# Hybrid macaron layer on one core: seven more seven-product units in the two feed-forward blocks, and the hidden tiles' splits moved

## The reference

```
h = x + 1/2 * SwiGLU_1(RMSNorm(x))
u = RMSNorm(h); P = u @ W_in
h = h + W_out(sigmoid(G_A) * (RWKV7(P) @ L_A) + sigmoid(G_B) * (DeltaNet(P) @ L_B))
h = h + CrossAttention(RMSNorm(h), RMSNorm(mem))
h = h + 1/2 * SwiGLU_2(RMSNorm(h))
y = RMSNorm_final(h)

SwiGLU(x) = (silu(n @ w_gate) * (n @ w_up)) @ w_down,  n = RMSNorm(x)
w_gate, w_up: 2048 x 5632     w_down: 5632 x 2048
```

## Time and profile before

| what | us |
|---|---|
| median of 3 runs | 2585.56 (2580.27 to 2589.16) |
| profiled execution, its own time | 2583.24 |
| its span, first to last instruction | 2581.5 |
| around the span | 1.74 |

### The profile page before, as it was taken

One profiled execution on the slowest core, in us unless ns is written; L12 is line 12 of the kernel. 1 busy time (PEld: TensorE's weight loads), 2 busy tenths in 40 slices (PEclk: granted clock), 3 DMA queues, 4 the chain that ended last, 5 costly groups with the idle time before them and its releaser, 6 DMA issues.

```text
span 2581.5 us, 34288 instructions
## 1 busy us (share of the span) xinstructions
PE 2553.0 (99%) x13611; PEld 2097.4 (81%) x13611; DVE 2019.9 (78%) x2403; ACT 1365.1 (53%) x1602; POOL 188.4 (7%) x346
## 2 busy tenths in 40 slices
PE   8999999999999999999999999999999999999998
PEld 7888888888888777878788888888888888888887
DVE  6999998887767796959666766555669999988876
ACT  5555555555456466446455544433555565555554
POOL 2000000000000011010001112000100000000000
PEclk9999999999999999999999999999999999999999
DMA  7767676667666675656478779644767676766655
GB/s 230 229 212 246 216 238 213 212 208 228 212 206 196 190 226 158 179 165 184 142 274 266 251 237 286 204 156 139 226 201 239 223 237 214 220 226 220 214 198 175
DMA packets 278576, 548.21 MB, mean 212 GB/s; under 512 B 25020, under 2 KB 35424, under 8 KB 278032
## 3 DMA queue, kind: packets, MB, share of 16 engines
q1 hardware_dynamic: 253904, 478.60, 58.1%
q0 software_dynamic: 24192, 66.89, 8.7%
q10 hardware_dynamic: 320, 0.53, 0.1%
HBM read 508.15 MB, written 37.77 MB: 211 GB/s over the span
## 4 chain that ended last, share of the span: by engine, by line
PE 69%; issue 16%; DVE 7%; DMA 4%; ACT 2%; POOL 1%; SPq 0%; DVEq 0%; POOLq 0%; ACTq 0%
PE pp L472 11%; PE pp L474 10%; PE pp L473 10%; PE pp L851 9%; PE pp L853 9%; PE pp L852 9%; DMA hid_dram<-hid_t 2%; DVE wlo L433 2%; POOL xq L735 1%; PE pb L851 1%; PE pb L853 1%; PE pb L852 1%; PE pa L852 1%; PE pa L851 1%; PE pa L853 1%
## 5 line engine op out<-in xcount | busy, mean ns | idle before, releaser
L433 DVE TENSOR_TENSOR wlo<-raw,whi 128x1024 fp32r<-128x1024 f32 (+1 forms) x676 | 812.3, 1216 | 310.5 <-ACT whi L428 294.0
L428 ACT ACTIVATE whi<-raw 128x1024 fp32r<-128x1024 f32 (+1 forms) x676 | 703.9, 1053 | 587.6 <-PE pp L474 438.4
L472 PE MATMUL pp<-whi,xhi 128*128 128x512 f32 (+1 forms) x928 | 371.3, 400 | 0.7 <-DVE xlo L590 0.7
L851 PE MATMUL pp<-whi,xhi 128*128 128x512 f32 x944 | 367.2, 389 | 0.0
L852 PE MATMUL pp<-whi,xlo 128*128 128x512 f32 x944 | 367.2, 389 | 0.0
L853 PE MATMUL pp<-wlo,xhi 128*128 128x512 f32 x944 | 367.2, 389 | 0.0
L474 PE MATMUL pp<-wlo,xhi 128*128 128x512 f32 (+1 forms) x928 | 360.2, 388 | 0.0
L473 PE MATMUL pp<-whi,xlo 128*128 128x512 f32 (+1 forms) x928 | 360.2, 388 | 0.0
L904 ACT ACTIVATE whi<-tw 128x1024 fp32r<-128x1024 f32 x156 | 165.6, 1062 | 286.3 <-PE pp L853 271.2
L922 DVE TENSOR_TENSOR wlo<-tw,whi 128x1024 fp32r<-128x1024 f32 x156 | 189.3, 1222 | 57.8 <-ACT whi L904 56.3
L851 PE MATMUL pp<-whi,hhi 128*128 128x512 f32 x572 | 223.0, 390 | 1.9 <-DVE wlo L433 1.9
(11 more groups left out here) (560 smaller groups left out, 4008.3 us busy)
## 6 DMA issues: line engine op xcount, KB each, us to landing
raw<-in_ffn_w_down SPq DMA_DIRECT2D x176, 512.0 KB, 4.7
raw<-in_w_in SPq DMA_DIRECT2D x144, 512.0 KB, 4.3
raw<-in_ffn_w_gate SPq DMA_DIRECT2D x134, 512.0 KB, 4.3
raw<-in_ffn_w_up SPq DMA_DIRECT2D x130, 512.0 KB, 4.8
raw_more<-in_ffn_w_up SPq DMA_DIRECT2D x46, 512.0 KB, 4.9
hid_dram<-hid_t POOLq DMA_DIRECT2D x43, 512.0 KB, 4.9
raw_more<-in_ffn_w_gate SPq DMA_DIRECT2D x42, 512.0 KB, 4.4
xq<-hid_dram POOLq DMA_DIRECT2D x156, 128.0 KB, 5.5
```

The lines of the kernel that those rows point to most:

```text
L428: nc.scalar.activation(hi_at(n)[:, :, 0:width], raw_at(r)[:, :, 0:width], ACT.Copy).then_inc(whi_ready, 1)
L433: nc.vector.tensor_tensor(lo_at(n)[:, :, 0:width], raw_at(r)[:, :, 0:width], hi_at(n)[:, :, 0:width].bitcast(F32), ALU.subtract).then_inc( ...
L472: nc.tensor.matmul(out, a_hi[:, k0 + k, tok], w_hi, start=first, stop=False)
L851: nc.tensor.matmul(out, a_hi, hi_at(n)[:, block, :], start=start, stop=False)
```

## The change

Chunk 9 joins WIDE. The pairs of the down product get 7, 6 (f1) and 7, 7 (f2) units, where they had 6, 4 and 6, 6; most come three plain slots apart in place of four. The fourth set of forms, for unit 6, has places of its own. Hidden tile 8 is split at the start of chunk 10, tile 9's low part at t = 0 of the down product, and TensorE waits for tile 9 inside q = 0, not ahead of it. Tile 10 is turned at t = 5, not 6, and its low part made at t = 10, not 12. A unit's first raw slot is free after its third sum, the second after the low part of w+1; its two raw places need not be neighbours any more (`wrapped`). The gains' load waits for the second unit of q = 1 of f2.

```diff
-WIDE = range(1, 9)
+WIDE = range(1, 10)
...
-DN_UNITS = {"f1": ((0, 1, 2, 3, 4, 5), (2, 3, 4, 5)), "f2": ((0, 1, 2, 3, 4, 5), (0, 1, 2, 3, 4, 5))}
-DN_AFTER = {"f1": ((5, 9, 13, 17, 21, 25), (5, 9, 13, 17)), "f2": ((5, 9, 13, 17, 21, 25), (1, 5, 9, 13, 17, 21))}
-DN_FORMS = {3: 0, 7: 1, 15: 2}
+DN_UNITS = {"f1": ((0, 1, 2, 3, 4, 5, 6), (0, 1, 2, 3, 4, 5)), "f2": ((0, 1, 2, 3, 4, 5, 6), (6, 0, 1, 2, 3, 4, 5))}
+DN_AFTER = {"f1": ((5, 8, 11, 14, 17, 20, 23), (3, 5, 8, 11, 13, 16)), "f2": ((5, 8, 11, 14, 17, 20, 23), (1, 4, 9, 12, 15, 18, 21))}
+DN_FORMS = {3: 0, 6: 1, 12: 2, 18: 3}
+HIDDEN_TURNS = (3, 5, 9, 10)
...
-        freed_by[r], freed_by[r + 1] = w + 2, w + 2
+        freed_by[r], freed_by[r + 1] = None, w + 1
...
+            elif since in summed_at:
+                sp.wait_ge(sem("sums_ready"), summed_at[since])
...
-            pe.wait_ge(x_ready, s0 + NFC - 1)
+            pe.wait_ge(x_ready, s0 + NFC - 2)
...
+                    for late in (0, 1):
+                        if q == 0 and pair["plain"][t][:2] == (pair["a"], FT // SK - 2 * (late + 1)):
+                            pe.wait_ge(x_ready, s0 + NFC - late)
...
+                    if t == 1 and i - 1 == WIDE[-1]:
+                        act.wait_ge(wlo_ready, gu[2 * i - 1]["done"])
+                        hidden_hi(act, tag, i - 2, hhi[:, 4 * i - 8:4 * i - 4, :])
-                    if t == gu_end(i) + 3:
+                    if t == gu_end(i) + 3 and i != WIDE[-1]:
                         hidden_hi(act, tag, i - 1, hhi[:, 4 * i - 4:4 * i, :])
...
+                    if t == 2 and i - 1 == WIDE[-1]:
+                        hidden_lo(dve, tag, i - 2, hhi[:, 4 * i - 8:4 * i - 4, :], hlo[:, 4 * i - 8:4 * i - 4, :])
...
+                    if q == 0 and t == 0:
+                        dve.wait_ge(sem("acts_ready"), ACTS[tag, "gu", NFC - 1, "gate"])
+                        hidden_lo(dve, tag, NFC - 2, hhi[:, 4 * NFC - 8:4 * NFC - 4, :], hlo[:, 4 * NFC - 8:4 * NFC - 4, :])
-                    if q == 0 and t == 6:
+                    if q == 0 and t == HIDDEN_TURNS[1]:
                         nat_turn(dve, None, nats[tag + "act"] + NFC - 1)
...
-            pool.wait_ge(slot_used, prods["f2dn"][0]["done"])
+            pool.wait_ge(slot_used, prods["f2dn"][2]["pair"]["units"][1][1] + UW)
```

More of the change, by code:

```diff
@@ L340, in build @@
         hs = {"f1": hs_f1, "f2": hs_f2}
-        whole = [at(f"whole{x}", kib, [4, T]) for x, kib in enumerate((193, AR + 84, 193))]
+        hs_more = {"f1": [at("hshi_more_f1", 64, [2, 4, P], F32R), at("hslo_more_f1", 80, [2, 4, P], F32R)],
+                   "f2": [at("hshi_more_f2", 64, [2, 4, P], F32R), at("hslo_more_f2", 68, [2, 4, P], F32R)]}
+        whole = [at(f"whole{x}", kib, [4, T]) for x, kib in enumerate((193, AR + 84, 193, 193))]
         nat = at("nat", 193, [TT, CW])
@@ L394, in loaded @@
             return LOADED[r_place[r]], load_counts[r]
+        summed_at = {}
+        for tag in ("f1", "f2"):
+            for mark, pr in [((tag, "gu", i), prods[tag + "gu"][2 * i]) for i in SEVEN] + [((tag, "dn", q), prods[tag + "dn"][2 * q]) for q in range(NDC // 2)]:
+                for j, _, r in pr["pair"]["units"]:
+                    summed_at[r] = SUMS[*mark, j, 3]
         def raw_free(sp, r):
@@ L844, in forms_lo, with units_of, unit_forms @@
             nc.vector.tensor_tensor(dst, src, hi.bitcast(F32), ALU.subtract).then_inc(sem("banks_free"), 1)
-        def units_of(x, n):
-            return x[:, 2 * n:2 * n + 2, :, :]
+        def units_of(tag, part, n):
+            return hs[tag][part][:, 2 * n:2 * n + 2, :, :] if n < 3 else hs_more[tag][part][:, :, :, :]
+        def unit_forms(tag, u):
+            return (hs[tag], u) if u < 6 else (hs_more[tag], u - 6)
         def product(out, a, n, block, start, stop):
@@ L853, in product, with wrapped @@
             return nc.tensor.matmul(out, a_hi, lo_at(n)[:, block, :], start=False, stop=stop)
+        def wrapped(r):
+            return r_place[r + 1] < r_place[r]
         def plain_pe(pe, pair, t, acts, tts=range(TT), used=1):
@@ L871, in unit_pe @@
         def unit_pe(pe, pair, n, acts, sums, u):
-            j, w, _ = pair["units"][n]
+            j, w, r = pair["units"][n]
+            swap = int(wrapped(r))
             first, final = n == 0, n == len(pair["units"]) - 1
@@ L891, in unit_pe @@
             pe.wait_ge(wlo_ready, w + 3)
-            product(M5, form(S_DIFF), w + 2, 0, first, final)
-            product(M7, form(S_CROSS), w + 2, 1, first, final).then_inc(slot_used, 1)
+            product(M5, form(S_DIFF), w + 2, swap, first, final)
+            product(M7, form(S_CROSS), w + 2, 1 - swap, first, final).then_inc(slot_used, 1)
             pe.wait_ge(wlo_ready, w + 4)
@@ L922, in lo @@
                 v.tensor_tensor(dst, src, hi.bitcast(F32), ALU.subtract).then_inc(wlo_ready, 1)
[L924 to L928, removed]
+            more = r_place[r] >= RING
+            assert more == (r_place[r + 1] >= RING)
+            blocks = (raw_more if more else raw)[:, :, :, :].rearrange("p s k n -> p (s k) n")
+            b11, b12 = [SK * (r_place[x] - more * RING) for x in (r, r + 1)]
+            b21, b22 = b11 + 1, b12 + 1
+            low, high = min(b11, b22), max(b11, b22)
             dve.wait_ge(*loaded(r))
@@ L931, in unit_dve @@
             dve.wait_ge(wlo_ready, w - 1)
-            v.tensor_tensor(tw[:, 0:2, :], blocks[:, b11:b22 + 1:3, :], blocks[:, b12:b12 + 1, :].to_broadcast([P, 2, CW]),
+            v.tensor_tensor(tw[:, 0:2, :], blocks[:, low:high + 1:high - low, :], blocks[:, b12:b12 + 1, :].to_broadcast([P, 2, CW]),
                             ALU.add).then_inc(sem("sums_ready"), 1)
@@ L935, in unit_dve @@
             dve.wait_ge(sem("sums_ready"), SUMS[*mark, j, 1])
-            v.tensor_tensor(tw[:, 2, :], tw[:, 0, :], blocks[:, b22, :], ALU.add).then_inc(sem("sums_ready"), 1)
+            v.tensor_tensor(tw[:, 2, :], tw[:, int(wrapped(r)), :], blocks[:, b22, :], ALU.add).then_inc(sem("sums_ready"), 1)
             lo(w + 1, lo_at(w + 1)[:, 0, :], blocks[:, b22, :], hi_at(w + 1)[:, 0, :])
@@ L1063, in ffn_act @@
                         x = DN_FORMS[t - 1]
-                        forms_hi(act, xs_dn[:, :, :, :], units_of(hs[tag][0], x), (tag, "dn", "forms", x))
-                    if q == 0 and t == 9:
+                        forms_hi(act, xs_dn[:, :, :, :], units_of(tag, 0, x), (tag, "dn", "forms", x))
+                    if q == 0 and t == HIDDEN_TURNS[2]:
                         hidden_hi(act, tag, NFC - 1, hhi[:, 4 * NFC - 4:4 * NFC, :])
@@ L1152, in ffn_dve @@
                         hidden_forms(0)
-                    if t == (gu_end(i) + 3 if i in WIDE else pair["na"] + 5):
-                        if i not in WIDE:
-                            dve.wait_ge(sem("acts_ready"), ACTS[tag, "gu", i, "gate"])
+                    if t == 2 and i - 1 == WIDE[-1]:
+                        hidden_lo(dve, tag, i - 2, hhi[:, 4 * i - 8:4 * i - 4, :], hlo[:, 4 * i - 8:4 * i - 4, :])
+                    if t == gu_end(i) + 3 and i < WIDE[-1]:
                         hidden_lo(dve, tag, i - 1, hhi[:, 4 * i - 4:4 * i, :], hlo[:, 4 * i - 4:4 * i, :])
@@ L1172, in ffn_dve @@
                         x = DN_FORMS[t - 1]
-                        forms_lo(dve, xs_dn[:, :, :, :], units_of(hs[tag][0], x), units_of(hs[tag][1], x), (tag, "dn", "forms", x))
-                    if q == 0 and t == 12:
+                        forms_lo(dve, xs_dn[:, :, :, :], units_of(tag, 0, x), units_of(tag, 1, x), (tag, "dn", "forms", x))
+                    if q == 0 and t == HIDDEN_TURNS[3]:
                         hidden_lo(dve, tag, NFC - 1, hhi[:, 4 * NFC - 4:4 * NFC, :], hlo[:, 4 * NFC - 4:4 * NFC, :])
```

6 lines of the change are left out of this document (2 added, 4 removed).

## The result

| | before | changed |
|---|---|---|
| median of 22 runs each, us | 2585.94 (2580.27 to 2592.54) | 2590.81 (2583.40 to 2597.59) |
| span of the profiled execution, us | 2581.5 | 2585.2 |

The ratio is 1.0019, 95% interval 1.0012 to 1.0026: the changed kernel is slower by 4.9 us (3.1 to 6.7). I had forecast 2585.1 us and no change. 2590.81 lies outside the 3.5 us that I had given to either side, and just inside the wider range up to 2591.0. That end was drawn for gains that land late, which did not happen, so lying inside it is luck. I had also held 7.8 us for the least that a measurement tells; 22 runs of each tell 4.9.

A forecast was written before the change was run, and what follows sets the result against it. TensorE was taken as the bound, busy 2553.0 of 2581.5 us, with VectorE nearly full. Terms of -4.76, -1.93, +2.9, +2.7 and +0.6 gave -0.5 us, a median of 2585.1 us; own range 3.5 us either side, wider range 2578.5 to 2591.0.

The forecast's parts named there:

- gains that land late: Rival, q = 1 of f2: load shares queues with weight loads, wait 6.4 us in place of 2.7, 2588.8 us; chance 0.10.
- Seven more units: Chunk 9 and down product of both blocks: each unit takes 24 matmuls to 21, -4.76 us if TensorE never waits.
- Sum: All terms, every one inside the feed-forward blocks, added: -4.76 - 1.93 + 2.9 + 2.7 + 0.6 = -0.5 us.
- The matmuls: Both feed-forward blocks: seven units save three matmuls each at 0.2266 us, -4.76 us.
- chunk 9: Gate and up, both blocks: VectorE's work rises to 39.8 us in 41.4, costed at nothing.
- The wait for tile 10: q = 0 of both down products: earlier turn removes TensorE's breaks of 1.04 and 0.89 us, -1.93 us.
- The forms: q = 0 of both blocks, t = 6, 12, 18: unit's third low part late by 0.48 us six times, +2.9 us.
- The gains' load: q = 1 of f2: VectorE stands until the load lands, 8.0 us after issue; TensorE waits at t = 8, +2.7 us.
- the covers: Rival: gains land in 5 us or so, VectorE comes early to the forms, no new wait: -6.7, 2578.9 us; chance 0.25.
- The tail: End of f2: two fewer plain slots after the last unit leave less cover for residual wait and final_gain, +0.6 us.
- The second raw slot: Rival, 20 gaps of three slots: weight loads land too late, 2595 us at a mean landing of 6.4; chance 0.10.

The follow-up runs named there:

- the third: Kernel before with 104 more semaphore instructions on TensorE, one per plain slot of f1's gate and up: 2585.51 us, ratio 1.0000.

## Why the prediction was wrong

**The step that failed is the sum's silent one.** "Seven more units" was costed as seven times three matmuls less, in the place where they go; that TensorE's stream becomes 22 instructions shorter for all that follows was costed at nothing, and "Sum" has no term outside the feed-forward blocks. The runs put some 5 us in its place (2.6 to 7 by the pair of kernels): with this placement the kernels that else differ by little are at 1.0019, 1.0024 and 1.0020, where before's placement and the third are at 0.9997 and 1.0000. That a shift of the stream makes the loss is shown, by adding it to before and taking it from the changed kernel; that the idles are waits for instruction packets is read from the fourteen traces. Bursts of small matmuls use the packets up fastest: 133 matmuls in the 6 us from 1050 to 1056, where steps of 0.2266 us make 26. Why a packet comes in time behind some short blocks and late behind others stays open: 107 arrive, and one to three idles are seen.

Inside the blocks the sum of -0.5 came out at -0.12, though its terms did not all hold. Over all matmul steps longer than 0.26 us in the two down stretches, the time above 0.2266 is 2.90 us before and 7.39 us in the changed kernel: -4.76 - 2.90 + 7.39 = -0.27. The old breaks were worth more than 1.93, and the new waits cost 7.4 where I had 6.2; of the 7.4 the waits below make 6.0, and slower steps right behind them the rest. That the sum came near is partly luck: the gains were put too high, and what was left out was nearly as much.

- **The matmuls, -4.76.** Right: 21 fewer. The two gate and up stretches gave 0.84 and 0.88 where the count gives 0.68 each, and chunk 9 cost nothing, as forecast: 41.50 us with VectorE busy 38.34 of it, where I had 39.8.

```profile
392.20:433.70 41.50, 41.50 (x185) 34.35 (x184) 38.34 (x40) 23.18 (x25) 2.75 (x5) 1.00 0.69 211
```

- **The wait for tile 10, -1.93.** Right in its mechanism: both breaks are gone. Too small: 1.63 + 1.44 = 3.07 us in the profile, 4.9 timed (2.6 to 7.2).
- **The forms, +2.9.** Three waits in each block, as forecast, but on the plain low part behind the sums; I followed the chain to the unit's third low part and left out the slot that TensorE asks for sooner. From one matmul to the next they cost 0.50, 0.59 and 0.50 us over the step, 3.2 us in both blocks: the size was near by luck.
- **The gains' load, +2.7.** One wait where I had it, on the low part of t = 8; it cost 1.2 us, as the load landed in 6.7 us and not in 8.0. VectorE's and TensorE's rows:

```profile
2490.71 1.23 DVE L1241 TENSOR_TENSOR h<-h,fgain 128x1024 f32<-128x1024 f32 x1 [4.89 <-DMA fgain<-in_final_norm]
...
2493.13 0.50 PE L865 MATMUL pp<-whi,hhi 128*128 128x512 f32 x1 [1.02 <-DVE wlo L444]
```

  I had the wait as L - 5.3. Over six executions L was 6.7, 6.7, 6.9, 7.6, 7.7 and 8.0 and the wait 1.02, 1.10, 1.29, 1.95, 2.08 and 2.41: L - 5.6, so the mechanism holds and the constant was off by 0.3. None of these landings came near the 4.4 us that I had estimated from the Trainium skill (DMA: Bandwidth & Descriptors, Anatomy of one DMA — SWDGE (gpsimd) path); here the trace decides, and the covers did not hold.
- **The tail, +0.6.** One wait of 0.30 us, 0.46 with its slow step.
- **Missed: +1.1 at t = 16 of q = 1 in f1.** I had not seen that the last unit now meets eight low parts of the next stage's input there. They stand on VectorE (2.19 us) between the unit and the next slot's low part:

```profile
664.94 1.23 DVE L941 TENSOR_TENSOR wlo<-tw,whi 128x1024 fp32r<-128x1024 f32 x1 [0.86 <-ACT whi L923]
666.08 2.19 DVE L797 SCALAR_TENSOR_TENSOR xlo<-xq,prm,xhi 128x128 fp32r<-128x128 f32 x8
668.19 2.35 DVE L444 TENSOR_TENSOR wlo<-raw,whi 128x1024 fp32r<-128x1024 f32 x2
```

- **The rivals.** The gains landed neither early nor very late. The second raw slot was late at times (0.59 and 0.60 us in two executions), far from the 20 gaps that would have decided.

## What to carry to other kernels

Before costing an edit at nothing outside its own lines, look whether it changes the number of instructions on the bound engine ahead of bursts of small ones: a shift alone was worth 5 us here, as much as the matmuls of seven units. It can be told from the edit's own worth by adding instructions that do nothing to both kernels. And where a unit is moved next to other work on VectorE, follow every slot that TensorE asks for behind that work, not only the unit's own parts; moving the sums behind a second plain slot took those waits away. Time the cheapest part of an edit by itself, too: here one line was worth 4.9 us, and the rest some 2 on top of it.

## What had not been expected of the hardware

TensorE sat idle for up to 2.9 us in the midst of matmuls until a packet of its own instructions had landed, at a place that moved with the number of instructions ahead of it: 26 idles in fourteen traces, all at number 192 or 193 of 256. And 208 instructions that only tested a semaphore cost nothing in a stretch of large matmuls (410.96 us with, 411.12 without). At or right behind 16 of the 19 idles of 1.5 us and more, and six waits of 2.1 to 2.9 us, the granted clock stood at half for 3.4 or 6.8 us.
